# Moving a last normalisation, a wait of GpSimd and the context's squares in a one-core transformer kernel

## The reference

```
def layer_norm(x, g, b):
    mu = mean(x); var = mean(square(x - mu))
    return (x - mu) * rsqrt(var + 1e-5) * g + b

# sub-layer 0, the multi-head one: latent tokens and context tokens are both normalised
h_l = rmsnorm(x,   norm1_g) * (1 + sc1)  + sh1
h_c = rmsnorm(ctx, norm1_g) * (1 + csc1) + csh1

# sub-layers 4 to 9 (second block); the last one is a feed-forward layer, and its
# layer_norm is the output of the whole program
y = (silu(gate(h)) * up(h)) @ w_out
x = layer_norm(alpha * x + 0.5 * (1 + gate2) * y, g, b)
```

## Time and profile before

| | |
|---|---|
| Time, median of 3 runs | 2126.3 us (2124.29 to 2126.75) |
| The profiled execution | 2124.72 us, of which 2122.9 us span |
| PE busy | 2084.2 us, 98% of the span |
| DVE, ACT, POOL busy | 60%, 20%, 23% |
| Mean granted clock of PE | 0.991 |
| HBM read | 434.20 MB, 206 GB/s |

### The profile page before, as it was taken

One profiled execution on the slowest core, in us unless ns is written; L12 is line 12 of the kernel. 1 busy time (PEld: TensorE's weight loads), 2 busy tenths in 40 slices (PEclk: granted clock), 3 DMA queues, 4 the chain that ended last, 5 costly groups with the idle time before them and its releaser, 6 DMA issues.

```text
span 2122.9 us, 24027 instructions
## 1 busy us (share of the span) xinstructions
PE 2084.2 (98%) x9428; PEld 1675.1 (79%) x9428; DVE 1272.6 (60%) x2509; ACT 422.6 (20%) x804; POOL 495.0 (23%) x411
## 2 busy tenths in 40 slices
PE   7999999999999999999999999999999999999997
PEld 4777888688876887687788888688868868888865
DVE  5546588746776466746523687777776653346554
ACT  3334211022110111033130311031102323122101
POOL 0100244402543244300000144414440000002340
PEclk9999999999999999999999999999999999999998
DMA  9673576775768564842334475766574333444431
GB/s 376 248 268 98 201 285 244 275 264 204 298 241 297 200 245 188 293 166 103 155 124 154 160 281 236 273 235 242 227 256 174 131 154 119 159 158 159 153 134 70
DMA packets 61551, 437.85 MB, mean 206 GB/s; under 512 B 6976, under 2 KB 8768, under 8 KB 40448
## 3 DMA queue, kind: packets, MB, share of 16 engines
q1 hardware_dynamic: 28608, 317.82, 38.8%
q0 software_dynamic: 32256, 117.45, 15.8%
q10 hardware_dynamic: 576, 1.05, 0.1%
HBM read 434.20 MB, written 2.10 MB: 206 GB/s over the span
## 4 chain that ended last, share of the span: by engine, by line
PE 88%; DVE 7%; DMA 2%; POOL 1%; issue 1%; ACT 1%; SPq 1%; ACTq 0%; DVEq 0%; POOLq 0%
PE lin L1881 27%; PE small_ps L2027 18%; PE lin L2027 13%; PE small_ps L2089 5%; PE lin L2122 5%; PE lin L2089 4%; PE small_ps L1881 3%; PE lin L2353 3%; PE pstat L2004 1%; PE lin L2278 1%; DVE proj L1131 1%; DVE ada_ring L1095 1%; PE small_ps L2372 1%; DMA ada_ring<-in_ada 1%; DMA rec<-in_ada_pe 1%
## 5 line engine op out<-in xcount | busy, mean ns | idle before, releaser
L1881 PE MATMUL lin<-h,ring 128*128 128x256 f32 x1968 | 434.2, 382 | 4.4 <-ACT h L1000 2.4
L1881 PEld LDWEIGHTS lin<-h,ring 128*128 128x128 f32 x1968 | 373.9, 191 | 60.1 <-issue 8.8
L630 POOL TENSOR_TENSOR proj<-ring 128x1024 f32<-128x1024 f32 x54 | 127.8, 2366 | 836.6 <-DVE xc L1310 633.4
L1095 DVE CUSTOM_DVE_ANT_0 ada_ring<-ada_ring,crow 128x1024 f32<-128x1024 f32 x224 | 265.9, 1220 | 32.9 <-DMA ada_ring<-in_ada 32.5
L615 POOL DMA_DIRECT2D ada_ring<-in_ada x224 | 121.4, 542 | 702.3 <-DVE sums L1095 667.8
L2027 PE MATMUL small_ps<-ring,h 128*128 128x256 f32 x864 | 195.6, 379 | 4.8 <-DVE sq L1112 4.8
L2027 PEld LDWEIGHTS small_ps<-ring,h 128*128 128x128 f32 x864 | 163.8, 190 | 28.4 <-issue 6.2
L2027 PE MATMUL lin<-proj,sq 128*128 128x256 f32 x672 | 153.9, 379 | 0.0
L2027 PEld LDWEIGHTS lin<-proj,sq 128*128 128x128 f32 x672 | 127.7, 190 | 17.4
L1881 PE MATMUL lin<-rec,ring 128*128 128x258 f32 (+2 forms) x608 | 139.5, 380 | 0.0
L1881 PEld LDWEIGHTS lin<-rec,ring 128*128 128x128 f32 x608 | 115.2, 190 | 16.8
(11 more groups left out here) (428 smaller groups left out, 3038.0 us busy)
## 6 DMA issues: line engine op xcount, KB each, us to landing
ring<-in_w SPq DMA_DIRECT2D x66, 2048.0 KB, 8.9
ada_ring<-in_ada POOLq DMA_DIRECT2D x224, 512.0 KB, 5.9
ring<-in_w2a SPq DMA_DIRECT2D x30, 1536.0 KB, 7.7
ring<-in_gates SPq DMA_DIRECT2D x12, 2048.0 KB, 8.0
ring<-in_w2d SPq DMA_DIRECT2D x12, 1408.0 KB, 7.3
ring<-in_mproj SPq DMA_DIRECT2D x8, 2048.0 KB, 7.9
ring<-in_mtok SPq DMA_DIRECT2D x4, 2048.0 KB, 8.2
ring<-in_branch SPq DMA_DIRECT2D x4, 2048.0 KB, 7.6
```

The costliest lines, as they stand in the source:

```text
L630: W(combined_weights(j, 0), b12, b11, ALU.subtract).then_inc(s_weights_combined, 1)
L1095: V.tensor_tensor_reduce(w, w, crow[:, 0 if s < FIRST2 else 1], 1.0, 0.0, ALU.mult, ALU.add, sums[:, s % 3, b:b + 1]).then_inc(s_ada_used, 1)
L1881: ins = mm(dst, w[:, lo:lo + m], rhs(k), start=k == 0, stop=k == nk - 1)
```

## The change

Three edits, one diff.

- POOL's first pair of differences in a folded feed-forward layer waits for the added squares (`s_squares_added`) in place of the scaled tiles; its waits for the second raw unit and for the weights stay.
- The context's squares are added up by DVE from eight tiles to two, PE makes two ones-products in place of eight and makes them after the first unit's second half. One of DVE's two `ada` blocks comes after the additions.
- The last normalisation is rebuilt. The first seven tiles are centred by the mean over these seven, squared and added up while PE still works on the last unit; for this PE makes one ones-product in the middle of that unit. When the eighth tile comes, it is centred by the same value, and the true mean and variance follow from two sums, each with one ones-product. The missing part of the mean is added to the tiles by DVE (four tiles) and POOL (four tiles), the root's table is loaded ahead, and ACT writes six output tiles, DVE two.

```diff
@@ gpsimd, combine
                     if folded(ph.name[0]):
-                        pool.wait_ge(s_x_scaled, tiles_scaled(ph.name[0]))
+                        pool.wait_ge(s_squares_added, folds_before(ph.name[0] + 1))
@@ gpsimd, at the end
+            pool.wait_ge(s_x_centred, 4 * (len(subs) - FIRST2) + 3)
+            for k in (4, 6):
+                mean = sq[:, 3].unsqueeze(1).broadcast_to([P, 2, T])
+                nc.gpsimd.tensor_tensor(xc[:, k:k + 2], xc[:, k:k + 2], mean, ALU.add).then_inc(s_final_centred, 1)
@@ scalar, at the end
-            fold_in(len(subs), None)
-            for k in range(KD):
+            for k in range(0, KD - 2, 2):
+                act.wait_ge(s_x_centred, nth(act, s_x_centred))
+                A(sq[:, k:k + 2], xc[:, k:k + 2], ACT.Square).then_inc(s_fold_squares, 1)
+            act.wait_ge(s_x_centred, nth(act, s_x_centred))
+            A(sq[:, KD - 2], xc[:, KD - 2], ACT.Square).then_inc(s_fold_squares, 1)
+            A(lbv[:, 0, 0:1], eps[:, 1:2], ACT.Sqrt)
+            act.wait_ge(s_x_centred, nth(act, s_x_centred))
+            A(sq[:, KD - 1], xc[:, KD - 1], ACT.Square).then_inc(s_fold_squares, 1)
+            act.wait_ge(s_final_mean_taken, 1)
+            A(sq[:, 2], sq[:, 3], ACT.Square).then_inc(s_final_square, 1)
+            act.wait_ge(s_final_variance, 1)
+            A(sd[:], sq[:, 4], ACT.Sqrt, bias=eps[:, 1:2]).then_inc(s_deviation, 1)
+            for k in range(FINAL_BY_ACT):
@@ vector
+            most = (KD - 1) * P
+            final_sum, final_squares = yab[:, 0], yab[:, 1]
+            def final_first_tiles():
+                dve.wait_ge(s_mean_sums, nth(dve, s_mean_sums))
+                for k in range(0, KD - 2, 2):
+                    V.scalar_tensor_tensor(xc[:, k:k + 2], pa[2][:, 0:T].unsqueeze(1).broadcast_to([P, 2, T]), -1.0 / most,
+                                           x[:, k:k + 2], ALU.mult, ALU.add).then_inc(s_x_centred, 1)
+                V.scalar_tensor_tensor(xc[:, KD - 2], pa[2][:, 0:T], -1.0 / most, x[:, KD - 2],
+                                       ALU.mult, ALU.add).then_inc(s_x_centred, 1)
+                V.scalar_tensor_tensor(final_sum, pa[2][:, 0:T], -1.0 / P, rstd[:], ALU.mult, ALU.add).then_inc(s_dve_chain, 1)
+                dve.wait_ge(s_fold_squares, nth(dve, s_fold_squares, 4))
+                for n, (a, b) in enumerate(((sq[:, 0:2], sq[:, 2:4]), (sq[:, 0:2], sq[:, 4:6]), (sq[:, 0], sq[:, 1]))):
+                    V.tensor_tensor(a, a, b, ALU.add).then_inc(s_dve_chain, 1)
+                    dve.wait_ge(s_dve_chain, nth(dve, s_dve_chain, 1 if n else 2))
+                V.tensor_tensor(final_squares, sq[:, 0], sq[:, KD - 2], ALU.add).then_inc(s_dve_chain, 1)
+            def final_last_tile(u):
+                dve.wait_ge(*taken(u))
+                V.scalar_tensor_tensor(xc[:, KD - 1], pa[2][:, 0:T], -1.0 / most, x[:, KD - 1],
+                                       ALU.mult, ALU.add).then_inc(s_x_centred, 1)
+                dve.wait_ge(s_x_centred, nth(dve, s_x_centred))
+                V.tensor_tensor(final_sum, final_sum, xc[:, KD - 1], ALU.add).then_inc(s_final_parts, 1)
+                dve.wait_ge(s_fold_squares, nth(dve, s_fold_squares))
+                V.tensor_tensor(final_squares, final_squares, sq[:, KD - 1], ALU.add).then_inc(s_final_parts, 1)
+            def final_norm():
+                dve.wait_ge(s_final_mean, 1)
+                V.tensor_scalar(sq[:, 3], pstat[:, 0:T], -1.0 / D, None, ALU.mult).then_inc(s_final_mean_taken, 1)
+                for k in (0, 2):
+                    V.tensor_tensor(xc[:, k:k + 2], xc[:, k:k + 2], mean, ALU.add).then_inc(s_x_centred, 1)
+                    if k == 0:
+                        dve.wait_ge(s_final_square, 1)
+                        dve.wait_ge(s_final_squares, 1)
+                        V.scalar_tensor_tensor(sq[:, 4], pa[3][:, 0:T], 1.0 / D, sq[:, 2],
+                                               ALU.mult, ALU.subtract).then_inc(s_final_variance, 1)
+                make_rstd(rstd[:])
+                for k in range(KD):
+                    if k % 2 == 0 and k >= 4:
+                        dve.wait_ge(s_final_centred, k // 2 - 1)
+                    V.tensor_tensor(xc[:, k], xc[:, k], rstd[:], ALU.mult).then_inc(s_x_scaled, 1)
...
+                for k in range(FINAL_BY_ACT, KD):
...
+                    V.tensor_scalar(x[:, k], xc[:, k], vec[:, g:g + 1], vec[:, b:b + 1], ALU.mult, ALU.add).then_inc(s_final_tiles, 1)
@@ vector, residual
-                    if s >= FIRST2 and m:
+                    if s + 1 == len(subs) and m == KD - 1:
+                        final_last_tile(u0 + m)
+                    elif s >= FIRST2 and m:
...
+                    if s + 1 == len(subs) and m == KD - 2:
+                        final_first_tiles()
@@ vector, multi-head
-                    ada(ADA_BEFORE_CONTEXT)
+                    ada(ADA_BEFORE_CONTEXT - 1)
+                    dve.wait_ge(s_squares, KD)
+                    V.tensor_tensor(sq[:, 0:4], sq[:, 0:4], sq[:, 4:8], ALU.add).then_inc(s_context_squares, 1)
+                    dve.wait_ge(s_context_squares, 1)
+                    V.tensor_tensor(sq[:, 0:2], sq[:, 0:2], sq[:, 2:4], ALU.add).then_inc(s_context_squares, 1)
+                    ada(1)
@@ tensor, last feed-forward layer
+                        if s + 1 == len(subs) and m == KD - 1 and k == KF // 2:
+                            pe.wait_ge(s_tiles_added, nth(pe, s_tiles_added, KD - 2))
+                            mm(pa[2][:, 0:T], ones[:], rstd[:], start=True, stop=True).then_inc(s_mean_sums, 1)
@@ tensor, multi-head
                 tile_sum(b[:, 0:T], w, 0, KD, lat)
-                squares_summed()
                 tile_sum(b[:, T:2 * T], w, KD * P, KD, lat).then_inc(s_unit, 1)
+                pe.wait_ge(s_context_squares, 2)
+                for k in range(2):
+                    ins = mm(pstat[:, 0:T], ones[:], sq[:, k], start=k == 0, stop=k == 1)
+                ins.then_inc(s_sums_over_features, 1)
@@ tensor, at the end
-            mean_summed()
-            folded_squares_summed()
+            for n, done in enumerate((s_final_mean, s_final_squares)):
+                pe.wait_ge(s_final_parts, n + 1)
+                mm((pstat, pa[3])[n][:, 0:T], ones[:], yab[:, n], start=True, stop=True).then_inc(done, 1)
```

More of the change, by code:

```diff
@@ L72 @@
 CHUNKS = KF // 2 - RAW // 2
+FINAL_BY_ACT = 6
 PAIRS = [2, 2, 2, 2, 2, 1]
@@ L188, in build @@
         s_context_ready = sem("context_ready")
+        s_context_squares = sem("context_squares")
         s_conv_done = sem("conv_done")
@@ L291, in build @@
         s_base_made = sem("residual_base_made")
+        s_final_parts = sem("final_parts")
+        s_final_centred = sem("final_centred")
+        s_final_mean = sem("final_mean")
+        s_final_mean_taken = sem("final_mean_taken")
+        s_final_square = sem("final_square_of_mean")
+        s_final_squares = sem("final_squares")
+        s_final_variance = sem("final_variance")
+        s_final_tiles = sem("final_tiles")
         s_even_kept = sem("even_parts_kept")
@@ L594, in _ @@
             for k in range(0, KD, 2):
-                sp.wait_ge(s_x_new, k + 2)
+                if k < FINAL_BY_ACT:
+                    sp.wait_ge(s_x_new, k + 2)
+                else:
+                    sp.wait_ge(s_final_tiles, KD - FINAL_BY_ACT)
                 sp.dma_start(out[:, k:k + 2], x[:, k:k + 2]).then_inc(s_result_dma, 16)
@@ L1383, in prepare_residual @@
                     fold_gains(s + 1)
+            most = (KD - 1) * P
[8 more added lines that the diff above has]
+                V.scalar_tensor_tensor(final_sum, pa[2][:, 0:T], -1.0 / P, rstd[:], ALU.mult, ALU.add).then_inc(s_dve_chain, 1)
+                nth(dve, s_x_centred, 4)
+                dve.wait_ge(s_fold_squares, nth(dve, s_fold_squares, 4))
[3 more added lines that the diff above has]
+                V.tensor_tensor(final_squares, sq[:, 0], sq[:, KD - 2], ALU.add).then_inc(s_dve_chain, 1)
+                dve.wait_ge(s_dve_chain, nth(dve, s_dve_chain))
@@ new lines, in final_norm @@
+            def final_norm():
+                mean = sq[:, 3].unsqueeze(1).broadcast_to([P, 2, T])
+                dve.wait_ge(s_final_mean, 1)
+                V.tensor_scalar(sq[:, 3], pstat[:, 0:T], -1.0 / D, None, ALU.mult).then_inc(s_final_mean_taken, 1)
+                dve.wait_ge(s_final_mean_taken, 1)
+                for k in (0, 2):
[5 more added lines that the diff above has]
+                                               ALU.mult, ALU.subtract).then_inc(s_final_variance, 1)
+                dve.wait_ge(s_x_centred, nth(dve, s_x_centred, 2))
+                make_rstd(rstd[:])
[3 more added lines that the diff above has]
+                    V.tensor_tensor(xc[:, k], xc[:, k], rstd[:], ALU.mult).then_inc(s_x_scaled, 1)
+                dve.wait_ge(s_x_scaled, tiles_scaled(len(subs)) + KD)
+                for k in range(FINAL_BY_ACT, KD):
```

(5 more changed lines are left out.)

## The result

The changed kernel takes 2129.5 us (median of 16 runs, 2126.7 to 2133.1) against 2126.5 us of the kernel before in the same number of runs: ratio 1.0015, interval 1.0008 to 1.0022, so 3.2 us slower (1.7 to 4.7). The profiled execution has a span of 2127.6 us against 2122.9. The prediction said 2126.4 (2121.5 to 2130.5) and "same": the time is inside the range, 3.1 us above the forecast, and the difference is still under 0.2%.

What follows compares the result with a forecast made beforehand. PE, busy for 98% of the span, was taken as the limit except in the tail. +3.3 + 0.4 - 3.6 = +0.1 us gave 2124.8 us against the profiled execution, 2126.4 on the median; range 2121.5 to 2130.5.

Steps and rivals of the forecast that it cites:

- Part A: Feed-forward sub-layers 6, 7 and 9: POOL's earlier first sums hold DVE instructions longer and delay PE, +3.3 us.
- The rival in which POOL waits for DVE's run: Sub-layers 6, 7, 9: POOL's first sum gets in only behind DVE's tiles, costing nothing: 2123.1; chance 0.20, shared.
- that of no change: Same sub-layers: weights or unit hold POOL past 1200, so the edit costs nothing: 2123.1; chance 0.20, shared.
- Part B: Multi-head stage: the 2.7 us PE saves on the context's products turn into a 2.9 us wait, +0.4 us.
- Part C: Last normalisation at the end: the rebuilt tail ends the span at 2119.3 instead of 2122.9, -3.6 us.
- the reciprocal not held beside POOL: Tail: DVE's reciprocal runs unhindered beside POOL's sums; the rival, held, was +1.7 us, 2128.1, chance 0.10.
- the 2.3 us from last issue to end: End of the tail: the span was taken to end 2.3 us after the last store's issue, plus 0.3 shared transfer.
- the forecast's own range: Whole kernel: the time lies between 2124.5 and 2127.5 us if the forecast itself holds, chance 0.42.
- the clock rival: Multi-head stage: PE's clock falls to half in the new context wait, costing 3.4 us: 2129.8; chance 0.15.

Runs made afterwards that it cites:

- Part B alone: The kernel before with only the context's squares changed (DVE's two additions, two ones-products behind the first unit's second half): 1.0007, +1.5 us.
- everything together: The kernel before with POOL's first sums at the squares, two context products in their old place, new tail with DVE doing POOL's additions: 0.9960, -8.5 us.

## Why the prediction was right, and where a term was not

- **Part A, +3.3: right, +2.8 by the stages.** POOL started 3.3 us sooner after the unit (0.09 in place of 3.40). The hold is of the predicted form: one DVE instruction per POOL sum, first the second L1365, then the first L1338. The eight tiles ended 7.59 after the unit; by the sum's steps (0.09, 5.25, seven tiles at 0.34) it is 7.7. Price 0.98, 0.88 and 0.97 instead of 1.1. PE's wait came in two pieces, 1.16 and 1.15, where about 2.7 in two was said. The rival in which POOL waits for DVE's run, and that of no change, fall; with POOL's sums put where DVE has no such instruction the whole hold goes, and 1.7 us a place with it.
- **Part B, +0.4: right in kind, about +0.8.** The wait was 2.82 us against 2.9; the saved products turned into it. The clock did not fall in it in the change's profile (1.00 from 53 to 56). In the trace of Part B alone it did (half clock from 55.9 for 3.4 us), but the half-clock time ahead of 237 us was 13.7 in it, as in the kernels without the edit: one stretch had moved, none was added. The rival's +3.4 is not borne out; whether such a gap draws a stretch to it stays open.
- **Part C, -3.6: wrong, -1.0.** The steps held: the last unit taken 0.63 late (0.75 said), the reciprocal not held beside POOL (1.75), the tiles held 0.6 (0.8 said), the last store issued 4.3 us sooner. The step that failed is the last one, "the 2.3 us from last issue to end": it took the end of the program to be the stores' landing alone. POOL's closing DRAIN, 9.3 us after its last work, now ends 3.0 us after SP's; without POOL at the end the tail was 3.8 to 3.9 us shorter than before, near the forecast. What POOL's queue does in these 9.3 us no run shows. The trace of before shows this DRAIN, at 2070.5, and the prediction didn't ask what it would do if POOL worked last.
- **The sum.** +2.8 +0.8 -1.0 = +2.6 by the stages, +3.2 (1.7 to 4.7) by the time. The forecast +0.1 missed mainly the DRAIN's 3.0. The time lies outside the forecast's own range (2124.5 to 2127.5) and inside the wide one only because rivals of other kinds had opened it so far. It comes closest to the clock rival's 2129.8, whose mechanism added nothing in the traces. That the range held is luck as far as the tail goes.
- The Trainium skill (SBUF — State Buffer, "SBUF: two separate sides") was cited for an exclusive lock between VectorE and GpSimd. The traces agree with it for L1365 and L1338 (two SBUF inputs, held) and for the copies and L1333 with a PSUM input in the kernel before (0.15 to 0.48 us each from 1200.82 to 1201.89, beside POOL's sum of 1200.65: not held). The reciprocal has one SBUF input and kept 1.75 us beside POOL, in the changed tail and in the three sub-layers of the kernel with the early sums.
- Time and stages: for the kernels with the early sums the time says -8.1, -8.5 and -10.8 us (alone, in the change, with the tail) where their stages add up to -5.3, -5.5 and -9.1, and -8.5 with everything together, where its own trace adds up to -9.8. Each sum lies within the interval of the time or, for the first, at its edge (-10.8 to -5.3), so no further effect is shown. Whether an edit shifts the half-clock stretches or the waits for conditioning weights in a lasting way stays open.

## What to carry to other kernels

An earlier start of a helper engine is no gain in itself: ask beside which instructions of its neighbour it will lie, and put it beside idle time or PSUM work. GpSimd's two sums started 3.3 us earlier cost about 3 us over three places; started 8.9 us earlier, they gained 5.3. And before an engine is given work at the end of a program, look at how long its queue takes to close after its last work.

## What the runs showed of the hardware

- GpSimd's queue closes late: its DRAIN ended about 9.3 us after GpSimd's last instruction in every kernel here, whether that was a 1.0 us sum at 2072 us or a 0.2 us one at the very end. The DRAINs of VectorE and ScalarE ended within 0.1 us of their last instruction (before: tiles until 2118.80, DRAIN until 2118.85; 2120.53 and 2120.56). One 8-element addition there cost the program 6.6 us (4.0 to 9.1).
- Beside two GpSimd sums of 128x1024 (2.4 and 2.5 us), VectorE lost 4.3 us if it had nothing but instructions with two SBUF inputs, and nothing if it had a reciprocal and copies from PSUM.
- Stretches of half clock of 3.4 to 10.2 us turn up at slightly different places in each execution (before: 20.5 us of them ahead of the tail, after: 27.3) and move the time by some us. Waits of PE behind late conditioning weights near 670 to 700 and 900 us add 0 to 5.2 us more. A part worth 1 or 2 us was read from stages, not from medians.
